# Moving small multiplies of a two-block model from VectorE to ScalarE, with new shares of gathers per stage

## What is computed

```
# short convolution, width 3, per channel:
y_sc = (sb * causal_dwconv(sc * sx, conv_w)) @ w_out
# scan output of the mixer, normed per group of 256 channels:
yg = yg * rsqrt(mean(yg * yg) + EPS)            # 8 groups
# PEER: top 16 of 128 keys twice, top 16 of the sums; then
u = expert_u[eidx]; v = expert_v[eidx]          # gathers, 128 + 128 per token
act = gelu(einsum(xb, u)); out = einsum(softmax * act, v)
```

## Time and profile before

| | |
|---|---|
| median of 3 runs | 2611.59 us (2611.46 to 2615.94) |
| profiled execution | 2619.71 us |
| its span, first to last instruction | 2617.6 us, mean granted clock 0.918 |
| busy: PE / DVE / ACT / POOL | 2231.8 / 1540.7 / 686.2 / 1015.2 us |

### The profile page before, as it was taken

How to read it: one execution, slowest core, us unless ns; L and a number is a source line. 1 busy time by engine, 2 the same in 40 slices (tenths; PEclk the granted TensorE clock), 3 DMA queues, 4 the chain that set the end, 5 groups by cost and what they waited for, 6 DMA issues and landing times.

```text
span 2617.6 us, 31879 instructions
## 1 busy us (share of the span) xinstructions
PE 2231.8 (85%) x11894; PEld 1675.4 (64%) x11894; DVE 1540.7 (59%) x3675; ACT 686.2 (26%) x2063; POOL 1015.2 (39%) x1028
## 2 busy tenths in 40 slices
PE   7999889988659999799868753568979799999898
PEld 7998778987658888688534133323356555546595
DVE  3441186764798998966633678831047668676210
ACT  6662245621225555400100010011022100001220
POOL 0000003333324554445456655656644556572000
PEclk9999999999879999999889967679987899999999
DMA  6656658999778999799999989999989999998475
GB/s 232 219 210 224 251 216 331 402 373 413 297 302 306 387 395 338 288 401 414 370 361 410 368 324 362 385 358 369 382 329 342 361 400 393 415 406 319 138 285 206
DMA packets 186090, 869.27 MB, mean 332 GB/s; under 512 B 20800, under 2 KB 21056, under 8 KB 153680
## 3 DMA queue, kind: packets, MB, share of 16 engines
q0 software_dynamic: 147456, 536.94, 53.4%
q1 hardware_dynamic: 37904, 328.20, 32.4%
q10 hardware_dynamic: 576, 2.10, 0.2%
HBM read 865.06 MB, written 2.10 MB: 331 GB/s over the span
## 4 chain that ended last, share of the span: by engine, by line
PE 67%; DVE 19%; issue 5%; ACT 4%; DMA 2%; another core or an unknown queue 2%; DVEq 0%; ACTq 0%
PE ps L988 66%; DVE rows L2313 8%; DMA wr<-in_wso 1%; DVE si L1861 1%; ACT ynT L1613 1%; PE ps L1327 1%; DVE sv L1859 1%; DVE tmpx L1946 0%; DVE ci L1861 0%; DVE oh L2128 0%; DVE h L2334 0%; DVE ps L2334 0%; DVE oh L2122 0%; PE ps L1091 0%
## 5 line engine op out<-in xcount | busy, mean ns | idle before, releaser
L968 POOL DMA_INDIRECT rows<-in_pu,eidx x512 | 484.5, 946 | 986.4 <-DVE dots L2313 435.3
L2313 DVE CUSTOM_DVE_ANT_0 rows<-rows,ps 128x1024 f32<-128x1024 f32 x512 | 594.0, 1216 | 7.2 <-issue 6.6
L988 PE MATMUL ps<-uT,wr 128*128 128x128 f32 (+2 forms) x3456 | 553.9, 318 | 20.8 <-issue 10.4
L988 PEld LDWEIGHTS ps<-uT,wr 128*128 128x128 f32 x3456 | 503.7, 195 | 55.2 <-issue 17.7
L988 PE MATMUL ps<-hT,wr 128*128 128x128 f32 (+2 forms) x1600 | 371.1, 392 | 36.7 <-issue 33.4
L968 POOL DMA_INDIRECT rows<-in_pv,eidx x256 | 287.2, 1122 | 226.1 <-DVE h L2334 112.9
L988 PEld LDWEIGHTS ps<-hT,wr 128*128 128x128 f32 x1600 | 266.3, 203 | 137.7 <-issue 43.8
L968 POOL DMA_INDIRECT rows<-in_pv,eidxT x256 | 243.3, 950 | 151.2 <-issue 63.2
L988 PE MATMUL ps<-rows,wz 128*32 128x512 f32 x1024 | 207.7, 621 | 28.6 <-DMA rows<-in_pv,eidxT 18.7
L2334 DVE SCALAR_TENSOR_TENSOR h<-rows,wgt,h 128x1024 f32<-128x1024 f32 x128 | 163.7, 1279 | 7.6 <-DMA rows<-in_pv,eidx 4.1
L2334 DVE SCALAR_TENSOR_TENSOR ps<-rows,wgt,ps 128x1024 f32<-128x1024 f32 x126 | 161.7, 1283 | 5.5 <-issue 3.7
(11 more groups left out here) (411 smaller groups left out, 2841.8 us busy)
## 6 DMA issues: line engine op xcount, KB each, us to landing
wr<-in_wg SPq DMA_DIRECT2D x48, 1536.0 KB
wr<-in_wsc SPq DMA_DIRECT2D x24, 1536.0 KB
wr<-in_wso SPq DMA_DIRECT2D x24, 1536.0 KB
wr<-in_wgu SPq DMA_DIRECT2D x33, 1024.0 KB
wr<-in_wgate SPq DMA_DIRECT2D x24, 1024.0 KB
wr<-in_wqku SPq DMA_DIRECT2D x15, 1024.0 KB
wr<-in_wo SPq DMA_DIRECT2D x12, 1024.0 KB
wr<-in_wdn SPq DMA_DIRECT2D x8, 1536.0 KB
```

Source lines behind the costliest of these rows:

```text
L968: e.indirect_dma_start(ring[i % NR], None, A[table], bass.IndirectOffsetOnAxis(ap=index[:, t, k:k + 1], axis=0)).then_inc(gathered[i % NR] ...
L988: return e.matmul(o, l, r, start=start, stop=stop, skip_group_check=True)
L2313: e.tensor_tensor_reduce(row, row, wide[:], 1.0, 0.0, MUL, ADD, dots[:, k:k + 1]).then_inc(*dve.up(*u))
```

## The change

`times` loses on DVE the history in, the history out and the first tap; ACT does them, the history in with `keepx`, the other two in a part of its own in `times` behind a wait for DVE's product. The two other taps move from `times` to `short`, one position later, behind a wait for ACT's first tap. `ynorm` part 0 keeps the small inverse root on DVE; ACT scales the rows, seven instructions of 256 columns per tile, in `times` of j = 7. One conversion of 256 indices in `slots` replaces eight of 32 in `top`. `SX` goes from 1.6 to 1.1, the planner's costs of `times` and `short` change, and `QUOTA` has new numbers (their sum stays 1079).

```diff
--- before.py
+++ after.py
@@ -36,12 +36,12 @@
 SECOND = (("attend", 0, 2), ("attend", 2, 3), ("feed", 0, 3), ("attend", 3, 4), ("feed", 3, 4), ("out", 3, 4))
 VPE = (1, 2)
 VW = 1.5
-SX = 1.6
+SX = 1.1
 PLACES = ("early", "beside", "ring")
 CX = 3.1
 CY = 1.7
 AHEAD = 2
-QUOTA = {('mixer', 1, 1): 17, ('mixer', 1, 2): 19, ('late', 1): 6, ('sum', 1): 26, ('mixer', 2, 0): 66, ('mixer', 2, 1): 62, ('mixer', 2, 2): 39, ('sum', 2): 82, ('query', 2): 98, ('top', 3): 65, ('attend', 0): 142, ('heads', 0): 64, ('wout', 0): 42, ('attend', 2): 20, ('heads', 2): 19, ('wout', 2): 4, ('feed', 0): 20, ('feed', 0, 0): 28, ('feed', 0, 1): 34, ('feed', 0, 2): 49, ('down', 0, 0): 35, ('down', 0, 1): 100, ('top', 2): 0, ('query', 1): 14, ('late', 2): 20, ('feed', 0, 3): 8, ('top', 0): 0, ('mixer', 1, 0): 0}
+QUOTA = {('mixer', 1, 1): 21, ('mixer', 1, 2): 15, ('late', 1): 6, ('sum', 1): 26, ('mixer', 2, 0): 70, ('mixer', 2, 1): 62, ('mixer', 2, 2): 33, ('sum', 2): 82, ('query', 2): 96, ('top', 3): 65, ('attend', 0): 170, ('heads', 0): 40, ('wout', 0): 38, ('attend', 2): 20, ('heads', 2): 25, ('wout', 2): 6, ('feed', 0): 20, ('feed', 0, 0): 24, ('feed', 0, 1): 30, ('feed', 0, 2): 49, ('down', 0, 0): 35, ('down', 0, 1): 94, ('query', 1): 14, ('late', 2): 20, ('feed', 0, 3): 14, ('top', 0): 0, ('top', 1): 0, ('mixer', 1, 0): 0, ('top', 2): 4}
 
 
 class Rehearsal:
@@ -213,8 +213,8 @@
             pl.add("sprod", q, j, s_, p=mmc(n))
 
         return [(lambda: product(2), lambda: pl.add("keepx", q, j), None),
-                (lambda: product(1), lambda: pl.add("times", q, j, v=5 * vc(n)), None),
-                (lambda: product(0), lambda: pl.add("short", q, j, v=vc(n)), None)]
+                (lambda: product(1), lambda: pl.add("times", q, j, v=vc(n)), None),
+                (lambda: product(0), lambda: pl.add("short", q, j, v=3 * vc(n)), None)]
 
     def group_units(g):
         def product(s_):
@@ -1142,7 +1142,7 @@
                     m = M[q]
                     nt = group(*MIXERS[q])[0]
                     b = ps(*u)
-                    w.wait_ge(*dve.at("ynorm", q, j // 14))
+                    w.wait_ge(*(act.at("ynorm", q, 0) if j < 14 else dve.at("ynorm", q, 1)))
                     for c in range(nt):
                         x = e.transpose(b[:, 128 * c:128 * c + 128], m["yh"][:, c, 128 * j:128 * j + 128], ident)
                     x.then_inc(*pe.up(*u))
@@ -1531,9 +1531,34 @@
                     n = group(*MIXERS[q])[2]
                     b = bank[pl.bank["sprod", q, j, 2][0]]
                     w.wait_ge(*pe.at("sprod", q, j, 2))
+                    x = M[q][f"xp{xp_of['times', q, j]}"]
+                    if xp_from["times", q, j] is not None:
+                        w.wait_ge(*dve.at(*xp_from["times", q, j]))
+                    if q:
+                        w.wait_ge(*act.at("hsc", q - 1, j))
+                    e.activation(x[:, 0:2], hsc[:, j, :] if q else C["zero"][:, 0:2], ACT.Copy).then_inc(*act.up())
                     if j:
                         w.wait_ge(*dve.at("times", q, j - 1))
                     e.activation(M[q]["xs_"][:], b[:, 0:n], ACT.Copy).then_inc(*act.up(*u))
+
+                elif kind == "times":
+                    _, q, j = u
+                    m = M[q]
+                    nt, m0, n, nr, chunks = group(*MIXERS[q])
+                    x = m[f"xp{xp_of[u]}"]
+                    w.wait_ge(*dve.at("times", q, j))
+                    e.activation(hsc[:, j, :], x[:, n:n + 2], ACT.Copy).then_inc(*act.up("hsc", q, j))
+                    if j:
+                        w.wait_ge(*dve.at("short", q, j - 1))
+                    e.activation(m["tmpy"][:], x[:, m0:m0 + nr], ACT.Copy, scale=W["scw"][:, 3 * j:3 * j + 1]
+                                 ).then_inc(*act.up("first tap", q, j))
+                    if j == 7:
+                        w.wait_ge(*dve.at("yfactors", q))
+                        for c in range(nt):
+                            for g in range(7):
+                                yv = m["yh"][:, c, 256 * g:256 * g + 256]
+                                e.activation(yv, yv, ACT.Copy, scale=m["rs0"][:, 8 * c + g:8 * c + g + 1]
+                                             ).then_inc(*act.up("ynorm", q, 0))
 
                 elif kind == "slopes":
                     _, q, g = u
@@ -1951,32 +1976,26 @@
                     _, q, j = u
                     m = M[q]
                     nt, m0, n, nr, chunks = group(*MIXERS[q])
-                    x, cv, sw = m[f"xp{xp_of[u]}"], m["tmpy"], W["scw"]
+                    x = m[f"xp{xp_of[u]}"]
                     b = bank[pl.bank["sprod", q, j, 1][0]]
-                    then()
-                    if q == 0:
-                        e.memset(x[:, 0:2], 0.0).then_inc(*dve.up())
-                    else:
-                        e.tensor_copy(x[:, 0:2], hsc[:, j, :]).then_inc(*dve.up())
                     w.wait_ge(*act.at("keepx", q, j))
                     w.wait_ge(*pe.at("sprod", q, j, 1))
                     e.tensor_tensor(x[:, 2:2 + n], b[:, 0:n], m["xs_"][:], MUL).then_inc(*dve.up("times", q, j))
-                    then()
-                    e.tensor_copy(hsc[:, j, :], x[:, n:n + 2]).then_inc(*dve.up())
-                    e.tensor_scalar(cv[:], x[:, m0:m0 + nr], sw[:, 3 * j:3 * j + 1], None, MUL).then_inc(*dve.up())
+
+                elif kind == "short":
+                    _, q, j = u
+                    m = M[q]
+                    nt, m0, n, nr, chunks = group(*MIXERS[q])
+                    x, cv, sw = m[f"xp{xp_of['times', q, j]}"], m["tmpy"], W["scw"]
+                    b = bank[pl.bank["sprod", q, j, 0][0]]
+                    w.wait_ge(*act.at("first tap", q, j))
                     for k in (1, 2):
                         then()
                         e.scalar_tensor_tensor(out=cv[:], in0=x[:, m0 + k:m0 + k + nr],
                                                scalar=sw[:, 3 * j + k:3 * j + k + 1], in1=cv[:], op0=MUL, op1=ADD
                                                ).then_inc(*dve.up("tapped", q, j))
-
-                elif kind == "short":
-                    _, q, j = u
-                    m = M[q]
-                    nr = group(*MIXERS[q])[3]
-                    b = bank[pl.bank["sprod", q, j, 0][0]]
                     w.wait_ge(*pe.at("sprod", q, j, 0))
-                    w.wait_ge(*dve.at("tapped", q, j))
+                    then()
                     e.tensor_tensor(m["scT"][:, j, :], b[:, 0:nr], m["tmpy"][:], MUL).then_inc(*dve.up(*u))
 
                 elif kind == "xdt":
@@ -2029,11 +2048,13 @@
                     w.wait_ge(*act.at("yss", q, 7 if part else 6))
                     ss, rs, mean, a_ = y_norms(q, part)
                     rsqrt(rs, ss, mean, a_, 1.0 / 256, "y", q, part)
-                    g0, gn = (7, 1) if part else (0, 7)
+                    if part == 0:
+                        dve.mark("yfactors", q)
+                        continue
                     for c in range(nt):
-                        yv = m["yh"][:, c, 256 * g0:256 * (g0 + gn)].rearrange("p (g e) -> p g e", g=gn)
-                        e.tensor_tensor(yv, yv, b3(m["rs0"][:, 8 * c + g0:8 * c + g0 + gn], 256), MUL
-                                        ).then_inc(*dve.up("ynorm", q, part))
+                        yv = m["yh"][:, c, 1792:2048]
+                        e.tensor_tensor(yv, yv, m["rs0"][:, 8 * c + 7:8 * c + 8].to_broadcast([128, 256]), MUL
+                                        ).then_inc(*dve.up("ynorm", q, 1))
 
                 elif kind == "merged":
                     _, q, j = u
@@ -2073,8 +2094,6 @@
                     if h:
                         one, two = m["sv"][:, i, 2 * h - 2, :], m["sv"][:, i, 2 * h - 1, :]
                         cand = m["cand"][:, h % 2, :]
-                        e.tensor_copy(m["sif"][:, i, 2 * h - 2:2 * h, :], m["si"][:, i, 2 * h - 2:2 * h, :]
-                                      ).then_inc(*dve.up())
                         e.tensor_tensor(cand[:, 0:16], two, one[:, 0:1].to_broadcast([128, 16]), ADD
                                         ).then_inc(*dve.up())
                         e.tensor_tensor(cand[:, 16:72].rearrange("p (a b) -> p a b", a=7), b3(one[:, 1:8], 8),
@@ -2092,6 +2111,8 @@
                     gt = gate[:, t, :].rearrange("p (h k) -> p h k", h=8)
                     unit, place, last, second = (m[f"cy{i_}"] for i_ in range(4))
                     then()
+                    e.tensor_copy(m["sif"][:, i].rearrange("p h k -> p (h k)"), m["si"][:, i].rearrange("p h k -> p (h k)")
+                                  ).then_inc(*dve.up())
                     e.tensor_scalar(m["cu0"][:], m["ci"][:, i], 3, None, ALU.logical_shift_right).then_inc(*dve.up())
                     e.tensor_scalar(m["cu1"][:], m["ci"][:, i], 7, None, ALU.bitwise_and).then_inc(*dve.up())
                     then()
```

## The result

| | before | after |
|---|---|---|
| median of 22 runs each | 2619.88 us | 2628.49 us |
| lowest and highest | 2605.97 to 2630.93 | 2616.71 to 2638.69 |
| span of the profiled run, granted clock | 2617.6 us, 0.918 | 2633.4 us, 0.918 |
| busy PE / DVE / ACT | 2231.8 / 1540.7 / 686.2 | 2233.9 / 1520.1 / 699.3 us |

The ratio is 1.0033, with a 95% interval of 1.0018 to 1.0047: **slower, by some 8.6 us**. The forecast was 2608, faster by 3.8. DVE has 20.6 us less work and ACT 13.1 more; the kernel is slower all the same.

A forecast was written before the change was run, and what follows sets the result against it. PE bounds the kernel (67% of the last-ending chain), leaving mixer ends and gather stages; 2.7 - 3.0 + 0 + 0 - 0.5 - 7 + 4 = -3.8 takes 2619.7 to 2615.9, the median 8.1 lower: 2608 us, range 2601 to 2614.

The forecast's parts named there:

- attend 0: Tile 2's dots beside attend 0: pooled block and its wait leave, the moved PE work is hidden, -7 us.
- The slower rival: Tile 2's dots bound by gathers throughout, phase unchanged and 7.5 us of PE work added behind: 2619 us, chance 0.20.
- End of mixer 0, +2.7: Mixer 0's last step: ACT's seven row scalings come ahead of the Exp, +2.7 us (bounds -2.0 and +3.4).
- End of mixer 1, -3.0: Mixer 1's end: DVE loses row scaling, history, first tap and one dot; ACT's scalings lie behind the Exp, -3.0 us.
- End of mixer 2, 0: Mixer 2's end: DVE loses scaling and convolution work, but four more sums (4.8 us) stand there, 0.
- steady steps, 0: Mixers' steady steps: DVE loses two copies and a tap, ACT gains them, PE at 252.4 of 253 covers, 0.
- indices, -0.5: Choosing: one conversion of 256 columns replaces eight, -0.5 us over four tiles (bounds -1.6 and +1.2).
- heads of attend 2, +4: Attend 2's heads: 19 gathers become 25, six more dots on a busy DVE, +4 us (bounds 0 and +6.8).
- The rival of the scalings in all three ends: All three mixers' ends: ACT's scalings stand ahead of the Exp, ends give +7 instead of -0.3: 2615 us, chance 0.12.
- the much faster dots: Tile 2's dots shrink to their last third's pace, 1.42 us a dot: 2600 us, down to 2592, chance 0.24.
- The feed-forward, 0: Feed-forward: its shares fall by 4 and 4 and rise by 6 where PE is full, 0.

The follow-up runs named there:

- the three shares alone: Kernel before with only attend 0's three shares new (170, 40, 38 for 142, 64, 42): ratio 1.0034.
- round 3: Runs on the fourth chip, among them the changed kernel unchanged (1.0027) and the kernel before unchanged (2522.25 us).
- a_sx16: Changed kernel with the factor SX back at 1.6 instead of 1.1: ratio 1.0066 from 7 runs.
- a_taps_only: Changed kernel without the new shares, with SX 1.6 and the rows scaled on DVE: ratio 1.0003.
- round 2: Third chip; changed kernel with old shares from attend 0 on (1.0013), with old shares only ahead of it (1.0031), with only attend 0's three shares old (1.0001).
- a_rows_dve: Changed kernel with the scaling of the scan's rows back on DVE in all three mixers: ratio 1.0034.
- b_newshares: Kernel before with the new shares of gathers alone: ratio 1.0039.
- b_feed_new: Kernel before with only the new shares behind attend 2 (its heads and output, the feed-forward): ratio 0.999.

## Why the prediction was wrong, step by step

**The step that failed is attend 0**: "I take 7.5 for the pooled block and its wait, nothing for the rest, and hide what moves: -7". Measured, the two stretches that it speaks of need 6.5 us more in the changed kernel (361.9 to 368.5) and 9.1 more with the three shares alone; on the first chip 7.1 more (396.9 to 404.0). Both halves of the sentence were wrong. The first: the dots' stretch is paced by gathers (on the chip of round 3 DMA's share is 1.01 and one comes in some 1.40 us), so that what DVE no longer does there shortens it by 1.7 us at most, and in the changed kernel it is 3.0 longer, 1.9 of them by the place of one pooled block. The second: the PE work that leaves is not hidden, because the stretch behind it has PE at 94%; with the three shares alone it grows by 10.8 us. The amount of work was right (7.1 us left with the three shares, forecast 7.5). The slower rival had named the sign (phase unchanged, 7.5 us of PE work behind it) and the deciding point (above 186 us; the window has 190). That its 2619 lies as near to the result as it does is in part luck: on the first chip mixer 0's output also came 8.8 us later (298.2 to 307.0), the mixers' end to h3 of tile 1 was 13.4 shorter, and neither is in its sum. What should have told me is the pair in the earlier trace rows, 1.56 and 1.50 us a gather in two stretches with different users, which I set aside for one faster third. A slip beside it: the bounds as printed add up to -28 and +19 (+23 with the steady steps), not to the -22 and +16 that stand there.

**End of mixer 0, +2.7**: right in mechanism and in size of the instructions (seven in 2.90 us, forecast 2.8; the tap 0.39, forecast 0.4 with the history), too small as a sum. Between the sums of squares of groups 6 and 7 it is +7.2 us (13.6 to 20.8): 4.1 for the scalings, and 3.1 that stay with DVE's scaling, about what the lead falls behind the scan with the smaller SX (last `keepx` 6.2 us behind group 6's sum of squares instead of 3.2). With SX 1.6 the scalings cost 2.4 (18.1 in `a_sx16` for 15.7 in `a_taps_only`, on two chips). From the start of the kernel the last sum of squares is later by 7.6 us on the first chip, by 3.2 on the chip of round 3 and by 4.6 to 4.8 in the three kernels of round 2. Over all twenty traces it comes at 211.2 to 214.4 with ACT's scalings in mixer 0 and at 206.6 to 209.3 without. By the Trainium skill ("ScalarE: Activation LUTs", Rules for kernel authors) multiplies belong on VectorE. The trace agrees as to the price, 2.90 us on ACT for 2.02 on DVE; but by the runs the harm is done by their place ahead of the Exp, since behind it, in mixer 1, they cost and win nothing that shows (next paragraph).

**End of mixer 1, -3.0**: the end did get shorter, from 14.6 to 9.7 us between the last `keepx` and the last sum of squares. But not by what the forecast put first, the row scaling that leaves DVE: with that back on DVE (`a_rows_dve`) the end is 9.3 us, with SX at 1.6 and the scalings on ACT (`a_sx16`) 15.0. So it is mainly SX that shortens it (the new shares alone, in `b_newshares`, bring it to 12.1). And the lead's first `keepx` came later, 97.0 us behind mixer 0's output, for 91.1 and 94.1 before (92.9 in both kernels with ACT's taps and SX 1.6): a smaller SX moves the scan ahead of the lead. Between the two outputs 332.9 and 331.1 became 330.8, no gain that the spread of equal code (330.6 to 333.1 on three of the faster chips) doesn't cover. I had costed the end and not the beginning of the same shift.

**End of mixer 2, 0; steady steps, 0; indices, -0.5; heads of attend 2, +4**: borne out in their sum on the faster chips. From mixer 1's output to mixer 2's turned rows 447.3 became 446.7, within which the steps won 4 us (230.9 to 226.9 for six) and the end lost 5 behind the last sum of squares, where PE waits 9.8 instead of 5.0 us for h3 of tile 0: the four more sums of the forecast, 4.8 us. On the first chip the same part took 5.2 us more (456.7 to 461.9). On the way to h3 of tile 1 397.0 became 396.3; the logits took 4.1 to 4.2 us more in every kernel with the new shares of attend 2's heads. The rival of the scalings in all three ends is out by mixers 1 and 2, that of the much faster dots by the windows.

**The feed-forward, 0**: wrong on either chip, in opposite directions. On the first it takes 4.4 us more, on the second 4.6 to 8.6 (200.7 to 204.7 for 196.1); on the fast ones 1.1 more, but the down projection behind it 7.4 less, since a wait of PE of 6.1 us for DVE is gone. My windows of before came from the first chip, which doesn't have that wait.

One part of the profiled pair isn't the kernel's: in attend 3 the clock granted was lower in the changed kernel's run, and the stretch of tile 3's logits took 6.4 us longer (31.4 for 24.9; of the twenty traces one other has 31.4, `b_feed_new`, at a granted clock of 0.83 from 2340 to 2380 us, and eighteen have 24.9, the changed kernel's on the chip of round 3 among them). Windows of the changed kernel and, below, of before:
```profile
2412.00:2500.00 88.00, 80.90 (x432) 58.31 (x432) 20.34 (x83) 24.61 (x59) 0.00 (x0) 0.90 0.42 148
```
```profile
2401.00:2483.00 82.00, 75.06 (x438) 54.80 (x436) 20.80 (x84) 25.23 (x61) 0.00 (x0) 0.98 0.46 159
```
Without it the stretches differ by 9.4 us, near the 8.6 of the medians. Not taken apart is the 13 us that the first chip's changed kernel wins between mixer 2's turned rows and h3 of tile 1 (424.1 to 410.7); on the four faster chips it is 1. On the second chip this stretch takes 426.0 us in the changed kernel with the old shares, 412.1 and 413.2 in its two versions with the new ones, and 421.2 in the kernel before with the new ones: on these runs it takes the new shares and the changed code together, and slow gathers.

## What to carry to other kernels

Before work of one engine is moved out of a stretch, ask what sets the pace there. If it is another resource's rate (here a gather in 1.40 us), work that fills waits there is free, and taking it out puts it into the next stretch in which its engine is full (here 7.1 us out, 10.8 us more behind). Filling the stretch further won nothing here. Look at what then stands beside the last instruction of the stretch: one block there cost 1.9 us. A shift between two merged streams has a front as well as an end, and both are to be costed. And in an in-order engine an instruction's price is its place: the same seven scalings cost 4 us ahead of an Exp that others wait for, and nothing that shows behind it.

## What the runs showed of the hardware

**The chips differ by 4%, and not on TensorE.** The kernel before takes a median of 2620 and 2630 us on two chips and 2519 to 2520 on four. Steady steps with PE at 80 of 80 us are as long on either kind (19.6 us each in mixer 1); the difference is where DMA is busy throughout. The dots' stretch moves 356 GB/s on the second chip (changed kernel with the old shares) against 402 above:
```profile
1535.00:1742.00 207.00, 90.93 (x343) 72.34 (x343) 168.90 (x329) 19.67 (x50) 121.07 (x130) 0.66 0.92 356
```
The same 130 gathers take 1.59 us each there instead of 1.42. "DMA: Bandwidth & Descriptors" of the Trainium skill (Bandwidth, Measured) gives roughly 358 GB/s to each of two cores that stream from one memory, and 425 to a core alone. The two levels here are near these, but no run shows what a neighbour did. A sum that is right for one chip can thus have the wrong sign on another, as the feed-forward's had.

**ACT's small instructions overlap by about 0.09 us.** Seven of 256 columns, 0.49 us alone, take 2.90 us in a row, 0.41 each; the forecast had 0.40 from four smaller ones.
